# In-projection of a hybrid SSD and Hyena layer: change of half by contraction steps over four banks, operands split one by one, and the first weight tiles loaded a stage earlier

## The chip, the cores and the metric

One NeuronCore of a Trainium2 chip runs the whole layer as one program. The metric is the device time of one execution in microseconds (us), lower is better. The engines are TensorE (PE, with its weight loads as PEld), VectorE (DVE), ScalarE (ACT), GpSimd (POOL) and SyncE (SP), which here only issues DMAs. Each engine runs its own instructions strictly in the order of the program and meets the others through semaphores.

## The reference, cut to what matters

The layer normalises its input, multiplies it by one wide weight matrix (the in-projection), and feeds the columns to an SSD mixer and to a long convolution. Only the first three lines below are touched by the change.

```
h  = rmsnorm(x, norm_w) * (1.0 + scale) + shift          # x: 2048 tokens x 1024, f32
hc = rmsnorm(ctx, norm_w) * (1.0 + scale_c) + shift_c    # ctx: 256 tokens
cols = in_projection(h, w_in)                            # 1024 -> 9248 columns
...
y_m = mamba_mixer(cols["m_xbc"], cols["m_dt"], ...)      # width-3 convolution, chunked scan
y_h = hyena_mixer(cols["h_proj"], ...)                   # width-3 convolution, long convolution
out = x + gate * mixer_output(...)
```

## The kernel before

The in-projection (`phase_in_projection`, L513) is computed transposed: weight tiles of 128 output columns stand still in TensorE and 512 tokens stream past. The 2048 tokens are worked in two halves of 1024. A half is a list of NJ = 37 jobs, so `jobs` has 74; job NJ (number 37) is the first one of the second half. All jobs but one take a pair of weight tiles and one step of a Strassen-like scheme: seven products (`PAIR`, L519) instead of eight, each of a weight operand (A11, A12, S2, S3, S1, A22, S4: two plain halves first, the rest tiles or sums) with an operand of the tokens (B11, B21, T2, T3, T1, N4, B22: quarters of the normalised input and their sums and differences). A product has four contraction steps (k = 0 to 3, the constant KQ), and a step has three matmuls of 128x512: high by high (L715), low part of the tokens (L716), low part of the weights (L717), since every f32 operand is split into a rounded high part and the rest. So a pair job is 7 x 4 x 3 = 84 matmuls. The products go round four PSUM banks.

Who does what for a job: SP loads weight tiles into a ring of three (L648). POOL forms the four weight sums (L666 to L671) and then the low parts of all seven weight operands (L678). ACT rounds the high parts (`split`, L743), copies product 0 out of its bank (L808), and applies the closing function to the job before (`finish`, L753 and L763) and issues its store (L766). DVE adds up the other products (`take`, L843 to L859) and does the width-3 convolution of the job before (`conv`, L881 and L885). For jobs without a convolution (the last 16 of a half) `finish` runs when products 3 and 5 of the next job are done.

The token operands are made by the class `Operands` (L287), once per half and in four steps k: SP loads two row blocks of 128x1024 (`load`, L305) into one of two buffers; DVE multiplies by norm weight and by the rows of 1/rms, which lie in PSUM (`scale`, L311); ACT adds the shift (`shift`, L318); POOL forms T1, T3, T2 and N4 (`sums`, L328, L329, L331, L333); ACT rounds the high parts (`high`, L349) and DVE subtracts for the low ones (`low`, L354), both in three groups: B11, then B21 with B22, then the four sums as one instruction over 2048 columns.

For the first half this runs inside the norm stage (`phase_norm`, L357), between the context's own projection (L433). For the second half it runs inside the in-projection at job NJ, and there the raw rows lie in the buffer `pl_raw`, one set of which belongs to the even jobs and one to the odd, and the sums lie in the result buffers `pl_res`. So at job NJ every engine first ends the first half: the first load (SP, L305) waits for the `finish` of job NJ-2, the others for that of NJ-1; DVE and ACT wait until TensorE has done all products of job NJ-1; POOL waits for the last stores out of `pl_res`. TensorE takes product 0 of job NJ through k = 0 to 3, then product 1, and so on, and waits before each step for the group of the operand it needs (`PARTS` and `GROUP`).

Between stages the semaphores are cleared and all engines meet (`Phase.release`, L66 and L67). The first weight tiles of the in-projection are loaded after that meeting.

Of the kernel before, what the change touches and what calls it, by code (L numbers as in the profile page):

```python
# [18 lines left out]
F32 = mybir.dt.float32  # L19
# [267 lines left out]
class Operands:  # L287
# [4 lines left out]
    GROUP = (0, 1, 1, 2, 2, 2, 2)  # L292
    PARTS = 3
# [6 lines left out]

    def load(self, sp, k):
# [19 lines left out]
    def sums(self, pool, k):  # L321
        a, b = self.xb(k % 2, 0), self.xb(k % 2, 1)
        b11, b12, b21, b22 = a[:, 0:QW], a[:, QW:2 * QW], b[:, 0:QW], b[:, QW:2 * QW]
        t1, t2, t3, n4 = (self.tmp[:, i // 2, i % 2] for i in range(4))
        pool.wait_ge(self.s_norm, 2 * k + 2)
        if k:
            pool.wait_ge(self.s_lo, self.PARTS * k)
        self.nc.gpsimd.tensor_tensor(t1, b12, b11, ALU.subtract).then_inc(self.s_sum, 1)  # L328
        self.nc.gpsimd.tensor_tensor(t3, b22, b12, ALU.subtract).then_inc(self.s_sum, 1)  # L329
        pool.wait_ge(self.s_sum, 4 * k + 1)  # L330
        self.nc.gpsimd.tensor_tensor(t2, b22, t1, ALU.subtract).then_inc(self.s_sum, 1)  # L331
        pool.wait_ge(self.s_sum, 4 * k + 3)
        self.nc.gpsimd.tensor_tensor(n4, b21, t2, ALU.subtract).then_inc(self.s_sum, 1)  # L333

    def part(self, k, g):

        a, b = self.xb(k % 2, 0), self.xb(k % 2, 1)
        src = (a[:, 0:QW], b.rearrange("p (a n) -> p a n", a=2), self.tmp[:])[g]
        views = ((lambda o: o[:, 0, k, :]), (lambda o: o[:, 1:3, k, :]),
                 (lambda o: o[:, 3:7, k, :].rearrange("p (a b) n -> p a b n", b=2)))  # L340
        return src, views[g](self.hi), views[g](self.lo)

    def high(self, act, k, g):
        src, hi, lo = self.part(k, g)
        if g < 2:
            act.wait_ge(self.s_norm, 2 * k + g + 1)
        else:
            act.wait_ge(self.s_sum, 4 * k + 4)
        self.nc.scalar.activation(hi, src, ACT.Copy).then_inc(self.s_hi, 1)  # L349

    def low(self, dve, k, g):
        src, hi, lo = self.part(k, g)
        dve.wait_ge(self.s_hi, self.PARTS * k + g + 1)
# [3 lines left out]
def phase_norm(nc, t, keep, rs, op_hi, op_lo, xbc_c, dt_c):  # L357

    NW = 2 * KT + 1
    with ExitStack() as ctx:  # L360
# [9 lines left out]
        tmp = ph.sb("tmp", [P, 2, 2, QW])  # L370
# [7 lines left out]
                       lambda q, r: xb[:, q, r, :], tmp)  # L378
# [4 lines left out]
        def _(sp):  # L383
# [22 lines left out]
            for n in range(NW):  # L406
# [4 lines left out]
                if n in (4, 8):  # L411
                    ops.load(sp, n // 4 + 1)
            store(NW - 2)
# [23 lines left out]
        def _(act):  # L437
# [10 lines left out]
            for n in range(NW):  # L448
                act.wait_ge(s_mm, n + 1)
                if n < 2 * KT:  # L450
# [6 lines left out]
                    elif n % 4 == 1:  # L457
                        ops.high(act, k, 0)
# [2001 lines left out]
```

## Time and profile before

| what | us |
|---|---|
| median of 3 runs | 3803.88 (3801.89 to 3812.24) |
| profiled execution, its time | 3812.66 |
| profiled execution, its span | 3810.5 |
| in-projection in the span | 162.1 to about 1669 |
| TensorE busy in the span | 3419.6 (90%) |

All times of rows are positions in the span of the profiled execution. What lies around the span is 2.2 us. That execution is 8.8 us slower than the median, so differences are read off the profile and then taken from the median. A matmul's row shows a modelled duration: where matmuls follow one another what counts is the distance of their starts, which is 0.227 us at the full clock and 0.427 us at half of it.

### The profile page before, as it was taken

How to read it: one execution, taken by the hardware profiler on the slowest of the kernel's cores; microseconds unless marked ns; L12 is line 12 of the kernel's file. 1: busy time of each engine (PE TensorE's matmuls, PEld its weight loads, DVE VectorE, ACT ScalarE, POOL GpSimd, SP SyncE). 2: the span in 40 equal slices, each digit the busy share in tenths (PEclk: the TensorE clock that was granted, in tenths of full speed). 3: DMA queues.
4: the chain of work that ended last, by engine and by line, in shares of the span. 5: the costliest groups of instructions: out<-in, count | busy, mean ns of one | idle time of the engine just before them, and what ended most of it. 6: DMA issues, size and time to landing. Idle time of an engine off the chain costs nothing. (4 is left out here: it accounts for less than half of the span.)

```text
span 3810.5 us, 44950 instructions
## 1 busy us (share of the span) xinstructions
PE 3419.6 (90%) x16246; PEld 2827.6 (74%) x16246; DVE 2272.3 (60%) x2870; ACT 1523.0 (40%) x2933; POOL 1864.7 (49%) x1146
## 2 busy tenths in 40 slices
PE   6799999995999999966998999999577887999998
PEld 2678888884788888854996888887366776788886
DVE  5686885223778852227543666665576675567662
ACT  3423223334332223331775555454346553333332
POOL 0477998775869987721000101100257562445442
PEclk8899999997999999988999999999798998999999
DMA  7444333333343333358997857865594545556562
GB/s 255 154 139 143 116 111 111 111 111 110 105 143 106 111 111 111 111 201 345 279 298 201 186 129 172 183 158 130 178 376 144 161 137 186 171 194 209 184 200 100
DMA packets 406350, 636.47 MB, mean 167 GB/s; under 512 B 154731, under 2 KB 241691, under 8 KB 403091
## 3 DMA queue, kind: packets, MB, share of 16 engines
q1 hardware_dynamic: 305661, 442.22, 38.0%
q10 hardware_dynamic: 91256, 157.83, 11.3%
q0 software_dynamic: 9216, 33.56, 4.0%
q8 instruction: 132, 2.16, 0.3%
q14 instruction: 85, 0.70, 0.1%
HBM read 430.49 MB, written 203.03 MB: 166 GB/s over the span
## 5 line engine op out<-in xcount | busy, mean ns | idle before, releaser
L715 PE MATMUL pl_bank<-hl_hi,pl_a_hi 128*128 128x512 f32 x2056 | 811.9, 395 | 69.6 <-DVE hl_lo L354 47.0
L717 PE MATMUL pl_bank<-hl_hi,pl_a_lo 128*128 128x512 f32 x2056 | 804.2, 391 | 0.0
L716 PE MATMUL pl_bank<-hl_lo,pl_a_hi 128*128 128x512 f32 x2056 | 803.8, 391 | 0.0
L715 PEld LDWEIGHTS pl_bank<-hl_hi,pl_a_hi 128*128 128x128 f32 x2056 | 388.1, 189 | 152.8 <-DVE hl_lo L354 39.2
L678 POOL TENSOR_TENSOR pl_a_lo<-pl_sums,pl_a_hi 128x512 fp32r<-128x512 f32 x288 | 435.5, 1523 | 129.3 <-ACT pl_a_hi L743 129.2
L717 PEld LDWEIGHTS pl_bank<-hl_hi,pl_a_lo 128*128 128x128 f32 x2056 | 388.1, 189 | 82.2
L716 PEld LDWEIGHTS pl_bank<-hl_lo,pl_a_hi 128*128 128x128 f32 x2056 | 388.6, 189 | 78.5
L743 ACT ACTIVATE pl_a_hi<-pl_sums 128x512 fp32r<-128x512 f32 x288 | 181.9, 633 | 511.6 <-PE pl_bank L717 464.2
L2022 POOL TENSOR_TENSOR mo_w_lo<-mo_w,mo_w_hi 128x1024 fp32r<-128x1024 f32 x96 | 237.5, 2477 | 280.5 <-ACT mo_w_hi L2093 280.5
L678 POOL TENSOR_TENSOR pl_a_lo<-pl_w,pl_a_hi 128x512 fp32r<-128x512 f32 x220 | 306.8, 1408 | 102.6 <-ACT pl_a_hi L743 102.3
L2050 PE MATMUL mo_bank<-mo_hi,mo_w_hi 128*128 128x512 f32 x768 | 306.8, 400 | 23.4 <-POOL mo_w_lo L2022 18.6
L885 DVE SCALAR_TENSOR_TENSOR pl_res<-pl_raw,pl_taps,pl_res 128x1023 f32<-128x1023 f32 (+1 forms) x160 | 312.6, 1954 | 3.0
L2051 PE MATMUL mo_bank<-mo_lo,mo_w_hi 128*128 128x512 f32 x768 | 301.5, 393 | 0.0
L2052 PE MATMUL mo_bank<-mo_hi,mo_w_lo 128*128 128x512 f32 x768 | 301.4, 392 | 0.0
L1393 DVE TENSOR_TENSOR conv_prod<-conv_bank,conv_spec 128x512 f32<-128x512 f32 x256 | 173.1, 689 | 160.5 <-PE conv_bank L1286 132.2
L743 ACT ACTIVATE pl_a_hi<-pl_w 128x512 fp32r<-128x512 f32 x220 | 138.0, 629 | 293.2 <-PE pl_bank L717 284.5
L1346 ACT COPY conv_v<-conv_bank 128x256 f32<-128x256 f32 x256 | 154.2, 602 | 223.6 <-PE conv_bank L1297 223.6
L1205 POOL DMA_DIRECT2D conv_gin<-u_s x32 | 36.7, 1150 | 382.1 <-DVE conv_x L1358 382.1
L1198 POOL DMA_DIRECT2D conv_x<-u_s x16 | 18.6, 1162 | 385.6 <-POOLq L67 264.3
L2050 PEld LDWEIGHTS mo_bank<-mo_hi,mo_w_hi 128*128 128x128 f32 x768 | 145.4, 189 | 59.1 <-issue 18.5
L1111 DVE COPY spec_y<-spec_bank 64x256 f32<-64x256 f32 x256 | 109.4, 427 | 120.5 <-PE spec_bank L1085 118.5
L843 DVE TENSOR_TENSOR pl_raw<-pl_bank,pl_r 128x512 f32<-128x512 f32 x72 | 49.8, 692 | 209.7 <-PE pl_bank L717 183.5
(247 smaller groups left out, 7049.9 us busy)
## 6 DMA issues: line engine op xcount, KB each, us to landing
pl_w<-in_w_rec SPq DMA_DIRECT2D x146, 512.0 KB, 3.5
conv_spec<-spec_s SPq DMA_DIRECT2D x248, 256.0 KB, 6.0
mo_w<-in_w_br SPq DMA_DIRECT2D x96, 512.0 KB, 3.8
kern_s<-taps_res SPq DMA_DIRECT2D x16, 2048.0 KB, 7.0
spec_xin<-kern_s SPq DMA_DIRECT2D x64, 512.0 KB, 5.4
spec_s<-spec_res ACTq DMA_DIRECT2D x128, 256.0 KB, 4.0
st_xb<-tok_s SPq DMA_DIRECT2D x36, 768.0 KB, 7.2
g_s<-pl_res ACTq DMA_DIRECT2D x32, 512.0 KB, 3.0
```

The source lines that it names most:

```text
L678: nc.gpsimd.tensor_tensor(a_lo[:, n % NS, :], s, a_hi[:, n % NS, :].bitcast(F32), ALU.subtract).then_inc(s_lo, 1)
L715: pe.matmul(out, a_hi[:, q, m], op_hi[:, b, k, :], start=(i == 0 and k == 0), stop=False)
L716: pe.matmul(out, a_hi[:, q, m], op_lo[:, b, k, :], start=False, stop=False)
L717: mm = pe.matmul(out, a_lo[:, q, m], op_hi[:, b, k, :], start=False, stop=(i == len(terms) - 1 and k == KQ - 1))
L743: nc.scalar.activation(a_hi[:, n % NS, :], src, ACT.Copy).then_inc(s_hi, 1)
L885: nc.vector.scalar_tensor_tensor(out=dst, in0=src[:, i:i + width], scalar=taps[i], in1=dst, op0=ALU.mult, op1=ALU.add).then_inc(s_conv, 1)
L1346: nc.scalar.copy(v[:, :, k], bank[2 + k % 2][:, 0:CB]).then_inc(s_vm, 1)
L1393: nc.vector.tensor_tensor(prod[:, n % 4], bank[ubank[k % 4]][:, None, 0:CB].to_broadcast([P, 2, CB]), spec[:, n // 2 % SLOT, :, k % 2], AL ...
L2022: nc.gpsimd.tensor_tensor(w_lo[:, s % 3, :], w[:, s % 3, :], w_hi[:, s % 3, :].bitcast(F32), ALU.subtract).then_inc(s_wlo, 1)
L2050: pe.matmul(bank[s % 4][:], w_hi[:, q, m], hi[:, slot, k, :], start=(k == 0), stop=False)
L2051: pe.matmul(bank[s % 4][:], w_hi[:, q, m], lo[:, slot, k, :], start=False, stop=False)
L2052: mm = pe.matmul(bank[s % 4][:], w_lo[:, q, m], hi[:, slot, k, :], start=False, stop=(k == KT - 1))
```

## The change

Seven edits, all around the two seams of the in-projection (its start, and the change of half at job NJ):

1. The first two weight tiles go to a buffer outside both stages (`first`, `loaded`) and SP loads them near the end of the norm stage, ahead of its last two stores.
2. In job 0 POOL makes the low parts of A11 and A12 ahead of the four weight sums.
3. The token operands are split one at a time: seven `high` and seven `low` of 128x512 per step k, in the order of `ORDERS`, and each waits for its own sum only.
4. At job NJ TensorE takes products 0 to 3 together, step by step: step k = 0 of all four (into four banks), then k = 1, and so on. Products 4 to 6 follow as before.
5. `finish` of jobs without a convolution moves to products 0 and 1 of the next job.
6. Step k = 0 of the second half's operands moves ahead, into job NJ-1: load after the `finish` of NJ-2, `scale` behind product 3, `shift` behind product 4, splits behind products 5 and 6.
7. The sums lie in `pl_tok`, so that POOL waits for older stores. POOL does them for k = 0 between the low parts S3 and S1 of job NJ. A load may overwrite its buffer once the sums and the low part of B22 are done.

The core of the diff (the norm stage splits by the same rule and is left out):

```diff
@@ class Operands
     def load(self, sp, k):
         if k >= 2:
-            sp.wait_ge(self.s_lo, self.PARTS * (k - 1))
+            sp.wait_ge(self.s_sum, 4 * (k - 1))
+            sp.wait_ge(self.s_lo, self.count(k - 2, self.B22))
@@ phase_norm, SP
+            for i in range(2):
+                sp.dma_start(first["w"][:, i, :], t["w_rec"][T_XBC + i]).then_inc(first["s_w"][i], 16)
             store(NW - 2)
             store(NW - 1)
@@ phase_in_projection, SP
                 if J == NJ + 1:
                     sp.wait_ge(s_fin, fin0[NJ - 1])
                     ops.load(sp, 0)
                     sp.wait_ge(s_fin, fin0[NJ])
+                    sp.wait_ge(s_ed, ed0[NJ])
                     for k in range(1, KQ):
                         ops.load(sp, k)
@@ TensorE
+                if J == NJ:
+                    for k in range(KQ):
+                        for j in range(4):
+                            n = p0[J] + j
+                            (a, b), = prods[j]
+                            if k == 0:
+                                room(n)
+                                pe.wait_ge(s_lo, a0[J] + a + 1)
+                            mm = step(J, n, a, b, k, k == 0, k == KQ - 1)
@@ ScalarE
                 if J == NJ:
+                    act.wait_ge(s_mm, p0[NJ])
                     for m in order(J - 1):
                         finish(J - 1, m)
-                    act.wait_ge(s_mm, p0[NJ])
-                    ops.shift(act, 0)
...
+                    for i in (4, 5, 6):
+                        ops.high(act, 0, i)
+                    ops.shift(act, 1)
+                    for k in range(1, KQ):
+                        for i in range(5):
+                            ops.high(act, k, i)
                         if k + 1 < KQ:
                             ops.shift(act, k + 1)
-                        ops.high(act, k, 2)
+                        for i in (5, 6):
+                            ops.high(act, k, i)
...
+                    if J == NJ - 1:
+                        if j == 4:
+                            ops.shift(act, 0)
+                        for i in {5: (0, 1), 6: (2, 3)}.get(j, ()):
+                            ops.high(act, 0, i)
@@ VectorE
+                    if J == NJ - 1:
+                        if j == 3:
+                            ops.scale(dve, 0)
+                        for i in (0, 1, 2, 3) if j == 6 else ():
+                            ops.low(dve, 0, i)
```

ACT around the end of the first half, before: `pl_a_hi` are weight splits, L763 is `finish`, L318 `shift`, L349 `high`.

```order
453 L763 ACTIVATE pl_res<-pl_raw 128x1024
454 L766 DMA g_s<-pl_res 128x1024
455 L743 ACTIVATE pl_a_hi<-pl_sums 128x512
456 L763 ACTIVATE pl_res<-pl_raw 128x1024
457 L766 DMA g_s<-pl_res 128x1024
458 L763 ACTIVATE pl_res<-pl_raw 128x1024
459 L766 DMA g_s<-pl_res 128x1024
460 L318 ACTIVATE pl_raw<-pl_raw,keep_mod 128x1024 x2
461 L349 ACTIVATE hl_hi<-pl_raw 128x512
462 L349 ACTIVATE hl_hi<-pl_raw 128x2x512
463 L318 ACTIVATE pl_raw<-pl_raw,keep_mod 128x1024 x2
464 L349 ACTIVATE hl_hi<-pl_res 128x4x512
```

The same place now (L819 is `finish`, L324 `shift`, L369 `high`, L799 the weight split):

```order
455 L819 ACTIVATE pl_res<-pl_raw 128x1024
456 L822 DMA g_s<-pl_res 128x1024
457 L799 ACTIVATE pl_a_hi<-pl_sums 128x512 x3
458 L324 ACTIVATE pl_raw<-pl_raw,keep_mod 128x1024 x2
459 L799 ACTIVATE pl_a_hi<-hl_w 128x512
460 L369 ACTIVATE hl_hi<-pl_raw 128x512 x2
461 L799 ACTIVATE pl_a_hi<-pl_sums 128x512
462 L369 ACTIVATE hl_hi<-pl_tok 128x512 x2
463 L819 ACTIVATE pl_res<-pl_raw 128x1024
...
465 L819 ACTIVATE pl_res<-pl_raw 128x1024
...
467 L369 ACTIVATE hl_hi<-pl_tok 128x512 x2
```

The `shift` of k = 0 and four splits now stand among the weight splits of the last job of the half; the two closing `finish` stand between the splits of T1, T3 and those of T2, N4.

POOL at the same change of half, before: L678 makes low parts of weights, L328 to L333 the sums of a step.

```order
325 L678 TENSOR_TENSOR pl_a_lo<-pl_w,pl_a_hi 128x512 x2
326 L678 TENSOR_TENSOR pl_a_lo<-pl_sums,pl_a_hi 128x512 x3
327 L678 TENSOR_TENSOR pl_a_lo<-pl_w,pl_a_hi 128x512
328 L678 TENSOR_TENSOR pl_a_lo<-pl_sums,pl_a_hi 128x512
329 L328 TENSOR_TENSOR pl_res<-pl_raw 128x512
```

And now (L696 the low parts, L340 to L348 the sums):

```order
326 L696 TENSOR_TENSOR pl_a_lo<-pl_sums,pl_a_hi 128x512 x2
327 L340 TENSOR_TENSOR pl_tok<-pl_raw 128x512
328 L342 TENSOR_TENSOR pl_tok<-pl_raw 128x512
329 L345 TENSOR_TENSOR pl_tok<-pl_raw,pl_tok 128x512
330 L348 TENSOR_TENSOR pl_tok<-pl_raw,pl_tok 128x512
331 L696 TENSOR_TENSOR pl_a_lo<-pl_sums,pl_a_hi 128x512
332 L696 TENSOR_TENSOR pl_a_lo<-hl_w,pl_a_hi 128x512
333 L696 TENSOR_TENSOR pl_a_lo<-pl_sums,pl_a_hi 128x512
334 L340 TENSOR_TENSOR pl_tok<-pl_raw 128x512
```

The sums of k = 0 went ahead of three low parts; the sums of k = 1 to 3 follow after them.

POOL in job 0 of the in-projection, before and then now:

```order
32 L666 TENSOR_TENSOR pl_sums<-pl_w 128x512
33 L668 TENSOR_TENSOR pl_sums<-pl_sums,pl_w 128x512
34 L669 TENSOR_TENSOR pl_sums<-pl_w 128x512
35 L671 TENSOR_TENSOR pl_sums<-pl_w,pl_sums 128x512
36 L678 TENSOR_TENSOR pl_a_lo<-pl_w,pl_a_hi 128x512 x2
```

```order
32 L696 TENSOR_TENSOR pl_a_lo<-hl_w,pl_a_hi 128x512 x2
33 L691 TENSOR_TENSOR pl_sums<-hl_w 128x512
34 L691 TENSOR_TENSOR pl_sums<-pl_sums,hl_w 128x512
35 L691 TENSOR_TENSOR pl_sums<-hl_w 128x512
36 L691 TENSOR_TENSOR pl_sums<-hl_w,pl_sums 128x512
```

The two low parts that TensorE's first two products need moved ahead of the four sums.

## Rows read from the trace of the kernel before

**Rows 1.** Windows: length, busy us (count) of PE, PEld, DVE, ACT, POOL, clock, DMA.

```profile
162.00:175.50 13.50, 0.00 (x0) 0.00 (x0) 0.38 (x11) 3.96 (x7) 6.30 (x6) 0.50 0.38 129
175.50:897.80 722.30, 717.87 (x3204) 591.85 (x3204) 421.51 (x447) 224.15 (x339) 593.54 (x403) 1.00 0.34 117
897.80:957.10 59.30, 12.34 (x34) 8.06 (x33) 30.61 (x22) 26.72 (x26) 30.78 (x20) 0.59 0.34 124
```

**Rows 2.** Waits, 897 to 975 us: total us, times, longest.

```profile
PE pl_bank L715 <- DVE hl_lo L354: 47.0, 5, 12.0
```

**Rows 3.** Waits of SP's queue, 880 to 1000 us.

```profile
SPq L305 <- ACT pl_res L763: 30.4, 2, 26.8
```

**Rows 4.** Timeline of PE, change of half: start, us, instruction, idle before and releaser.

```profile
897.60 0.39 PE L717 MATMUL pl_bank<-hl_hi,pl_a_lo 128*128 128x512 f32 x1
908.39 0.77 PE L715 MATMUL pl_bank<-hl_hi,pl_a_hi 128*128 128x512 f32 x1 [10.40 <-DVE hl_lo L354]
...
946.41 0.80 PE L715 MATMUL pl_bank<-hl_hi,pl_a_hi 128*128 128x512 f32 x1 [11.99 <-DVE hl_lo L354]
```

**Rows 5.** Timeline of the same stretch, the other engines.

```profile
884.43 0.69 DVE L843 TENSOR_TENSOR pl_raw<-pl_bank,pl_r 128x512 f32<-128x512 f32 x1 [4.75 <-PE pl_bank L717]
...
895.93 1.05 ACT L763 ACTIVATE pl_res<-pl_raw 128x1024 f32<-128x1024 f32 x1
...
903.34 2.47 DVE L311 SCALAR_TENSOR_TENSOR pl_raw<-pl_raw,keep_mod,rt_rows 128x1024 f32<-128x1024 f32 x2 [4.62 <-DMA pl_raw<-in_xT]
904.72 2.28 ACT L318 ACTIVATE pl_raw<-pl_raw,keep_mod 128x1024 f32<-128x1024 f32 x2 [3.33 <-DVE pl_raw L311]
...
907.55 0.69 DVE L354 TENSOR_TENSOR hl_lo<-pl_raw,hl_hi 128x512 fp32r<-128x512 f32 x1 [1.73 <-ACT hl_hi L349]
...
908.50 1.22 DVE L354 TENSOR_TENSOR hl_lo<-pl_raw,hl_hi 128x1024 fp32r<-128x1024 f32 x1 [0.25 <-ACT hl_hi L349]
...
910.82 1.27 POOL L329 TENSOR_TENSOR pl_res<-pl_raw 128x512 f32<-128x512 f32 x1
...
918.84 2.90 DVE L354 TENSOR_TENSOR hl_lo<-pl_raw,hl_hi 128x512 fp32r<-128x512 f32 x2
919.07 1.59 POOL L328 TENSOR_TENSOR pl_res<-pl_raw 128x512 f32<-128x512 f32 x1 [4.41 <-DVE hl_lo L354]
...
920.62 2.24 POOL L329 TENSOR_TENSOR pl_res<-pl_raw 128x512 f32<-128x512 f32 x1
...
971.88 0.69 DVE L859 TENSOR_TENSOR pl_raw<-pl_bank,pl_u 128x512 f32<-128x512 f32 x1 [2.03 <-PE pl_bank L717]
```

**Rows 6.** DMA issues in four short windows: KB each, us to landing.

```profile
xbc_c<-nl_res SPq DMA_DIRECT2D x1, 128.0 KB, 4.6
...
dt_c<-nl_res SPq DMA_DIRECT2D x1, 128.0 KB, 1.8
...
pl_ident<-in_ident SPq DMA_DIRECT2D x1, 64.0 KB, 2.6
...
pl_raw<-in_xT SPq DMA_DIRECT2D x2, 512.0 KB, 5.4
```

**Rows 7.** Timeline, norm stage to in-projection.

```profile
162.98 18.93 SPq L648 DMA_DIRECT2D pl_w<-in_w_rec  x5
167.72 1.15 ACT L743 ACTIVATE pl_a_hi<-pl_w 128x512 fp32r<-128x512 f32 x2 [8.72 <-DMA pl_w<-in_w_rec]
169.12 1.26 POOL L666 TENSOR_TENSOR pl_sums<-pl_w 128x512 f32<-128x512 f32 x1 [19.64 <-DMA pl_w<-in_w_rec]
...
175.53 0.76 PE L715 MATMUL pl_bank<-hl_hi,pl_a_hi 128*128 128x512 f32 x1 [22.63 <-POOL pl_a_lo L678]
...
181.64 0.40 PE L717 MATMUL pl_bank<-hl_hi,pl_a_lo 128*128 128x512 f32 x1
```

**Rows 8.** Source lines L67 and L66: duration ns min/median/max, first and last start.

```profile
L67 SPq EVENT_SEMAPHORE  x10: 17/17/17, 81.6 to 3810.5; - x10
...
L66 POOLq DRAIN  x10: 58/98/121, 81.0 to 3809.8; - x10
```

More of the change, by code:

```diff
@@ L664, in _ @@
+                if not J:
+                    low(A11, half[0][0])
+                    low(A12, half[0][1])
                 if len(job.tiles) == 2:
-                    n = 4 * pairs[J]
-                    nc.gpsimd.tensor_tensor(sums[:, 0], wt[1][:, 0:QW], wt[1][:, QW:D], ALU.add).then_inc(s_sum, 1)
+                    total(0, half[1][0], half[1][1], ALU.add)
                     pool.wait_ge(s_sum, n + 1)
-                    nc.gpsimd.tensor_tensor(sums[:, 1], sums[:, 0], wt[0][:, 0:QW], ALU.subtract).then_inc(s_sum, 1)
@@ L675, in _ @@
-                for i, s in enumerate(src):
-                    n = a0[J] + i
-                    pool.wait_ge(s_hi, n + 1)
-                    nc.gpsimd.tensor_tensor(a_lo[:, n % NS, :], s, a_hi[:, n % NS, :].bitcast(F32), ALU.subtract
-                                            ).then_inc(s_lo, 1)
+                    total(3, half[0][1], sums[:, 1], ALU.subtract)
+                if J:
+                    low(A11, half[0][0])
+                    low(A12, half[0][1])
+                if len(job.tiles) == 2:
+                    low(S2, sums[:, 1])
+                    low(S3, sums[:, 2])
+                    if J == NJ:
+                        for q in range(2):
+                            pool.wait_ge(s_tst[q], 16 * stores_before(t0[NJ] + q))
+                        ops.sums(pool, 0)
+                    low(S1, sums[:, 0])
+                    low(A22, half[1][1])
+                    low(S4, sums[:, 3])
@@ L700, in _, with room, step @@
             pe.wait_ge(s_ident, 16)
-            for J, prods in enumerate(products):
+            def room(n):
+                if n >= 4:
+                    engine, count = freed[n - 4]
+                    pe.wait_ge(s_ea if engine == "act" else s_ed, count)
+            def step(J, n, a, b, k, begin, end):
+                out, q, m = bank[n % 4][:], (a0[J] + a) % NS, slice(k * P, (k + 1) * P)
+                if J == NJ:
+                    pe.wait_ge(ops.s_lo, ops.count(k, b))
+                pe.matmul(out, a_hi[:, q, m], op_hi[:, b, k, :], start=begin, stop=False)
+                pe.matmul(out, a_hi[:, q, m], op_lo[:, b, k, :], start=False, stop=False)
+                return pe.matmul(out, a_lo[:, q, m], op_hi[:, b, k, :], start=False, stop=end)
@@ L810, in _ @@
                         split(J + 1, j)
[L811 to L814 removed]
+                    if J and J != NJ:
+                        for m in order(J - 1):
+                            if j == (5 - 2 * m if jobs[J - 1].conv is not None else 1 - m):
+                                finish(J - 1, m)
+                    if J == NJ - 1:
[3 more added lines that the diff above has]
+                            ops.high(act, 0, i)
                     if j == 2 and J >= 2 and jobs[J - 2].turned:
```

152 lines of the change are left out of this document (81 added, 71 removed).

## The prediction

> **What bounds the kernel now.** I read the windows by stage first, then who waited for whom, then the timelines of the two stretches in which TensorE stands still. Within a half TensorE is the bound: between 175.5 and 897.8 us it is busy 717.87 of 722.30 us at the full clock, matmuls 0.227 us apart, while POOL is busy 82% of it and DVE 58% [rows 1]. No faster helper pays there. What can be saved lies at two seams.
>
> Seam A, the start: from 162.0 to 175.5 TensorE does nothing [rows 1]. The weights are issued at 162.98, ACT gets them at 167.72, POOL makes four sums from 169.12 and only then, near 174.1, the first low part, and the first matmul comes at 175.53, at half clock (0.427 us a matmul) until 181.64 [rows 7].
>
> Seam B, the change of half: the last matmul of the first half starts at 897.60 and ends its slot at 897.83 [rows 4]. The 84 matmuls of job NJ at 0.227 us would end 19.1 us later, at 916.9. The last product is taken by DVE at 971.88 [rows 5], so it ended at about 971.7: the seam costs 54.8 us. 47.0 us of it are five waits for DVE's low parts [rows 2], and the granted clock of the stretch is 0.59, the lower level while TensorE waits [rows 1]. It takes the steps k one after another because product 0 needs all four; they come at 908.39 to 946.41, 12.7 us apart [rows 4].
>
> **Seam A, part by part.** The first two tiles are already there when the stage opens, so what is left is: ACT's two high parts (0.65 us for the first; 1.15 for both [rows 7]), POOL's first low part (1.27, as a POOL subtraction without disturbance [rows 5]), and the identity matrix, on whose DMA TensorE waits ahead of everything: issued just ahead of the weights of 162.98, say 162.5, 2.6 us to landing [rows 6, 7], so 165.1. The first two end at 162.2 + 0.65 + 1.27 = 164.2; the identity is late next, so TensorE starts at 165.2 if the stage opens when it does now. The sums, now behind two low parts, are ready in time: POOL has low parts A11 at 164.2, A12 at 165.5, sums until 170.6, S2 at 171.9; TensorE wants S2 after 24 matmuls, 14 of them at half clock, 165.2 + 8.3 = 173.5. Cover: 1.6 us.
> The two weight loads stand ahead of the last two stores of the norm stage in SP's queue, and the stage ends when these have landed. Now they take 1.8 us; a store behind 1.5 MB of loads took 4.6 us [rows 6]. Here 1 MB is issued at about 156 and wants 5.4 us by the row of a pair of loads [rows 6], until 161.4; the last store, issued near 158.5, lands at about 161.8 instead of 161.2. I take a stage that opens 0.5 us later; bounds are 1 us earlier (one-by-one splits free DVE and ACT for the convolution before the last sooner, so the last stores go out sooner) and 2.5 us later (the 4.6 us in full). The splits themselves are the same work in more pieces, 28 instead of 12 on each engine, beside TensorE; I put them at nothing, with 1 us either way inside the same bounds.
> By the Trainium skill, DMA: Bandwidth & Descriptors, Queues, rings and completion order, descriptors of one issuing engine are consumed in ring order on each DMA engine. That speaks against putting the loads ahead of the stores; the 4.6 us row agrees with it, and the sum by the rule alone would be the late bound.
> Gain of seam A: 175.5 - 165.7 = 9.8 us (7.8 to 11.3). The cold start is the same in both.
>
> **Seam B, part by part.** Products end 2.72 us apart, product 1 of job NJ-1 at 884.4 [rows 5].
> 1. Load 0 waits for the second `finish` of NJ-2, now ended at 896.98 [rows 5]. At product 1 it ends at 884.4 + 0.65 (split) + 1.05 = 886.1. SP has stood there since 897.0 - 26.8 = 870 [rows 3], nothing else is queued ahead. The rows land 6.3 us later (897.0 to 903.34 [rows 5]) at 892.4.
> 2. `scale` takes 2.47, `shift` ends 3.7 after its start [rows 5]: 896.1. DVE stands for the load ahead of the take of product 4 (until 894.9 instead of 892.6); that bank is wanted again only by product 1 of job NJ, so nothing waits. POOL has low part S3 done at 892, makes T1 by 897.4 and T3 by 898.6.
> 3. DVE's low parts start behind its last take, 898.7, at 0.7 to 0.97 us: B11 by 899.6, B21 900.5, T1 and T3 by 902.3. TensorE works on products 0 and 1 there, 1.8 us after its end of the first half.
> 4. ACT's two closing `finish` (1.05 and a DMA issue, 1.5 each) stand ahead of T2: they run 899.9 to 902.5. T2 is split at 903.5, its low part is there at 904.3.
> 5. Load 1 waits for both: 902.5, landing 5.4 to 6.3 us later [rows 5, 6], 908.3. From here three steps are left, as now, but they no longer wait in series for one instruction of 2048 columns.
> 6. One step: `scale` and `shift` 3.7 us, then POOL. POOL and DVE disturb each other when both work on two SBUF operands: DVE's two instructions took 2.90 us at 918.84 where 0.69 + 1.22 = 1.9 is undisturbed, and POOL's two beside them 1.59 + 2.24 instead of 2 x 1.27; beside L311, whose one operand is in PSUM, POOL keeps its 1.27 (910.82) [rows 5]. So each loses about half of the overlap. Step 1: normalised at 912.0, T1 and T3 made after 2.54 + 1.4 = 916.0, T3 rounded at 916.7, then `shift` of step 2 (2.3) until 919.3. N4 of step 1 is made by 918.6; only then may load 3 go, 5.4 us, 924.0; behind DVE's five low parts `scale` starts 924.5, and step 3 is normalised at 928.2. T1, T3, T2 of it take 3.8 + 2.1, the high and the low part 1.3: T2 of step 3 is there at 935.4. The pitch is 8.1 us instead of 12.7.
> 7. TensorE has then 6 + 36 matmuls left. It has had bursts of 3 to 6 between waits, so I take the lower clock, which the whole stretch shows now (0.59 granted on the mean [rows 1]), and for as long as after 175.53: 6.1 us, 14 matmuls [rows 7]: 14 x 0.427 + 28 x 0.227 = 12.3 us. End at 947.8 instead of 971.7.
> Gain of seam B: 23.9 us. Bounds: with no disturbance at all the last T2 comes at 931.5 (gain 28); with today's pitch of 12.7 for steps 2 and 3, behind T2 of step 1 at 920.8, at 946.2 (gain 13). The value taken is the one whose terms are rows of this stretch.
> By the Trainium skill, GPSIMD Engine Reference, its specification table, the two engines contend when DVE has two SBUF inputs; the rows of point 6 agree. Were it a full exclusion, 4.2 + 5.1 = 9.3 us a step, the gain would be about 21.
>
> What is queued behind: POOL turns to job NJ+1 at about 936.3 and has A11 after four sums and a low part, 6.6 us, 942.9; TensorE wants it at 947.8. Cover 4.9 us (now 11). In steady jobs POOL has slack, and TensorE never waits for it, so the lead grows back. The earlier `finish` costs ACT 2.64 us in product 0's 2.72 us, ahead of nothing TensorE waits for. I put both at nothing.
> **A new cost:** the weight semaphores now belong to an outer group, which had none, so one more clear and meeting stands behind the in-projection: 81.0 to 81.6 [rows 8], 0.6 us.
>
> **Sum:** -9.8 - 23.9 + 0.6 = -33.1 us. From the profiled execution 3812.66 that gives 3779.6. It was 8.8 us above the median of the runs, so for the median I say 3803.88 - 33.1 = 3770.8.
>
> **Rivals.** (a) The pitch stays: splits one by one bring more instructions and semaphore trips, POOL and DVE fill the time, steps come 12.7 us apart. For it: DVE and ACT waited for each other in every step. Against: most of each step now is idle, DVE is busy 30.6 of 59.3 us [rows 1]. -9.8 - 13 + 0.6 = 3781.7.
> (b) Both better than taken: disturbance and stage end cost nothing, 28 + 11.3 - 0.6: 3765.2.
> (c) The preload pays little: the last stores wait behind the weights and the identity behind them, seam A gives 5: 3775.6.
> (d) Slower: POOL, which comes out of seam B with 4.9 us of lead instead of 11, does not regain it in the 20 jobs with a convolution, and sets their pace. It decides from 33.1/20 = 1.7 us a job; at 2.3 us the time is 3817. Against: in the first half the same jobs start with little lead and TensorE lost 4.4 of 722 us [rows 1].
>
> **How the numbers follow.** The forecast 0.74, (a) 0.12, (b) 0.07, (c) 0.04, (d) 0.03. The forecast's own terms give 3766 to 3779, and the median of a few runs moves by some us (the three lie 10 apart). I take 3763 to 3784, which holds (a), (b) and (c). Faster by over 0.3% (11 us, about what a measurement of this kernel tells from no change) 0.96, same 0.01, slower 0.03.
>
> **What would show it.** First matmul of the in-projection at 165 to 167; load 0 issued near 886; TensorE in pairs of bursts, the last long wait ending near 935; end of job NJ near 948; waits for the low parts of the tokens in that stretch 20 to 27 us instead of 47; no waits for POOL in jobs NJ+1 to NJ+3. I am wrong if load 0 is late, so that DVE delays the takes, if the steps keep 12.7 us, or if the norm stage ends over 2 us later.

## The result, and the profile after

The changed kernel takes 3788.04 us (median of 5, 3785.08 to 3793.64) against 3804.16 of the kernel before beside it: ratio 0.9950, interval 0.9939 to 0.9961, so 15 to 23 us less. The forecast was 33 us less, 3770.8, and its range ended at 3784. The sign was right and the size was not.

Windows of the changed kernel, as [rows 1]: opening of the in-projection to its first matmul, the first half, and from its end to the last long wait of TensorE.

```profile
160.90:163.41 2.51, 0.00 (x1) 0.00 (x1) 0.35 (x11) 1.15 (x2) 1.70 (x2) 0.50 0.49 101
163.41:886.10 722.69, 717.87 (x3204) 591.81 (x3204) 423.63 (x449) 230.00 (x348) 598.03 (x407) 1.00 0.35 120
886.10:935.00 48.90, 19.26 (x43) 10.74 (x43) 44.82 (x35) 25.22 (x38) 35.00 (x23) 0.64 0.34 118
```

The first half is what it was (722.7 us, 3204 matmuls). In the last window DVE is busy 44.8 of 48.9 us; before it was 30.6 of 59.3. TensorE's waits there, as [rows 2]:

```profile
PE pl_bank L750 <- DVE hl_lo L374: 29.6, 10, 6.0
```

Where the in-projection opens and ends, by the semaphore that lets SP out of the meeting between stages (first and last start), in the changed kernel:

```profile
L67 SPq EVENT_SEMAPHORE  x3: 17/17/17, 160.8 to 1649.0; - x3
```

Before, the same two meetings lie at 162.0 and 1673.2. The norm stage and the in-projection together took 1591.6 us and take 1568.7 now, 22.9 less; the new meeting costs 0.4 (1648.6 to 1649.0). All stages behind it took 2137.3 us and take 2136.3.

**Seam A.** Timeline of the changed kernel, as [rows 7]:

```profile
156.41 0.43 SPq L415 DMA_DIRECT2D dt_c<-nl_res  x1
...
160.91 1.15 ACT L799 ACTIVATE pl_a_hi<-hl_w 128x512 fp32r<-128x512 f32 x2 [4.89 <-PEq L67]
161.27 0.42 SPq L656 DMA_DIRECT2D pl_ident<-in_ident  x1
161.71 2.49 POOL L696 TENSOR_TENSOR pl_a_lo<-hl_w,pl_a_hi 128x512 fp32r<-128x512 f32 x2 [14.39 <-ACT pl_a_hi L799]
...
163.41 0.79 PE L750 MATMUL pl_bank<-hl_hi,pl_a_hi 128*128 128x512 f32 x1 [12.66 <-DMA pl_ident<-in_ident]
```

The identity matrix is what comes last, as forecast, and the first matmul comes 2.6 us after the stage opens instead of 13.5. The norm stage's last store, `dt_c`, takes 3.4 us to landing where it took 1.8, but it is issued 1.3 us sooner in its stage, so that the stage is 0.5 us longer.

**Seam B.** I count from the end of the first half (the first wait's end less its length: 887.70 - 1.47 = 886.2; before 908.39 - 10.40 = 898.0) to the start of DVE's take of the last product of job NJ. That was 971.88 - 898.0 = 73.9 us and is 61.4. Timeline of the changed kernel, DVE and POOL in the last step; L317 is `scale`, L374 `low`, L340 to L348 the four sums of the step, L691 and L696 weight sums and weight low parts of job NJ+1:

```profile
917.64 2.46 DVE L317 SCALAR_TENSOR_TENSOR pl_raw<-pl_raw,keep_mod,rt_rows 128x1024 f32<-128x1024 f32 x2
...
920.02 1.28 DVE L374 TENSOR_TENSOR hl_lo<-pl_tok,hl_hi 128x512 fp32r<-128x512 f32 x2
...
924.78 5.15 DVE L374 TENSOR_TENSOR hl_lo<-pl_raw,hl_hi 128x512 fp32r<-128x512 f32 x3
...
926.15 1.54 POOL L348 TENSOR_TENSOR pl_tok<-pl_raw,pl_tok 128x512 f32<-128x512 f32 x1
927.65 1.74 POOL L691 TENSOR_TENSOR pl_sums<-hl_w 128x512 f32<-128x512 f32 x1
...
929.47 1.59 POOL L691 TENSOR_TENSOR pl_sums<-pl_sums,hl_w 128x512 f32<-128x512 f32 x1
929.86 6.76 DVE L374 TENSOR_TENSOR hl_lo<-pl_tok,hl_hi 128x512 fp32r<-128x512 f32 x4
931.02 1.70 POOL L691 TENSOR_TENSOR pl_sums<-hl_w 128x512 f32<-128x512 f32 x1
932.69 1.71 POOL L691 TENSOR_TENSOR pl_sums<-hl_w,pl_sums 128x512 f32<-128x512 f32 x1
934.36 3.40 POOL L696 TENSOR_TENSOR pl_a_lo<-hl_w,pl_a_hi 128x512 fp32r<-128x512 f32 x2
...
936.55 0.68 DVE L907 TENSOR_TENSOR pl_raw<-pl_bank,pl_r 128x512 f32<-128x512 f32 x1
```

At 920.02 POOL rests and two low parts take 1.28 us. From 929.86 POOL works without a gap and four take 6.76, 1.69 each. POOL's instructions start 1.67 us apart there; earlier, beside nothing of DVE but takes out of PSUM, they start 1.25 us apart:

```profile
884.41 1.29 POOL L340 TENSOR_TENSOR pl_tok<-pl_raw 128x512 f32<-128x512 f32 x1 [4.23 <-ACT pl_raw L324]
885.66 1.28 POOL L342 TENSOR_TENSOR pl_tok<-pl_raw 128x512 f32<-128x512 f32 x1
```

A pair (one low part and one POOL instruction) takes 1.68 us. Both alone add up to 1.25 + 0.60 = 1.85, so only 0.17 us of the two overlap.

My theory after reading this, called **turn-taking** below: a DVE and a POOL instruction that both read two operands from SBUF do not share, they go one after the other, whole (but for these 0.17 us). The price of a low part beside a busy POOL is then one POOL instruction, whatever its own size, and splitting the operands one by one bought up to seven such turns in a step where there had been three. The rivals: the share goes by columns, as the forecast had it; ScalarE's highs or the loads set the pace; the interleaving over four banks, or the early freeing of the raw rows, carries the gain.

### The profile page after: what moved, and what is told of

It reads as the page before. It is cut to its first block and busy times, and to the rows that moved or that the text cites. A ratio compares the mean times of both kernels' runs of the same rounds, so it can differ in the third digit from the quotient of the medians.

```text
span 3785.4 us, 45041 instructions
## 1 busy us (share of the span) xinstructions
PE 3424.3 (90%) x16246; PEld 2828.8 (75%) x16246; DVE 2295.8 (61%) x2902; ACT 1525.8 (40%) x2965; POOL 1867.0 (49%) x1146
## 3 DMA queue, kind: packets, MB, share of 16 engines
q10 hardware_dynamic: 91256, 157.83, 11.2%
## 5 line engine op out<-in xcount | busy, mean ns | idle before, releaser
L750 PE MATMUL pl_bank<-hl_hi,pl_a_hi 128*128 128x512 f32 x2056 | 813.6, 396 | 42.3 <-DVE hl_lo L374 29.6
L696 POOL TENSOR_TENSOR pl_a_lo<-pl_sums,pl_a_hi 128x512 fp32r<-128x512 f32 x288 | 436.0, 1526 | 120.9 <-ACT pl_a_hi L799 120.9
L799 ACT ACTIVATE pl_a_hi<-pl_sums 128x512 fp32r<-128x512 f32 x288 | 181.8, 633 | 541.6 <-PE pl_bank L752 485.4
L696 POOL TENSOR_TENSOR pl_a_lo<-hl_w,pl_a_hi 128x512 fp32r<-128x512 f32 x220 | 309.8, 1422 | 115.5 <-ACT pl_a_hi L799 115.2
L2121 PE MATMUL mo_bank<-mo_hi,mo_w_hi 128*128 128x512 f32 x768 | 306.7, 399 | 22.5 <-POOL mo_w_lo L2093 18.4
L799 ACT ACTIVATE pl_a_hi<-hl_w 128x512 fp32r<-128x512 f32 x220 | 138.1, 629 | 259.1 <-PE pl_bank L752 253.2
L691 POOL TENSOR_TENSOR pl_sums<-hl_w 128x512 f32<-128x512 f32 x144 | 208.5, 1448 | 12.2 <-POOL pl_a_lo L696 12.2
L2121 PEld LDWEIGHTS mo_bank<-mo_hi,mo_w_hi 128*128 128x128 f32 x768 | 145.2, 189 | 58.7 <-issue 18.6
```

Source lines behind the costliest of these rows:

```text
L691: nc.gpsimd.tensor_tensor(sums[:, i], x, y, op).then_inc(s_sum, 1)
L696: nc.gpsimd.tensor_tensor(a_lo[:, at % NS, :], src, a_hi[:, at % NS, :].bitcast(F32), ALU.subtract).then_inc(s_lo, 1)
L750: pe.matmul(out, a_hi[:, q, m], op_hi[:, b, k, :], start=begin, stop=False)
L799: nc.scalar.activation(a_hi[:, n % NS, :], src, ACT.Copy).then_inc(s_hi, 1)
L2121: pe.matmul(bank[s % 4][:], w_hi[:, q, m], hi[:, slot, k, :], start=(k == 0), stop=False)
```

## Experiments

Time ratios are to the kernel before on the same chip. Norm stage and in-projection are the stages' lengths in the profile, in us. "Last wait" is the start of the matmul behind TensorE's last wait for a low part, and "seam B" the end of job NJ, both from the end of the first half. Stops under 0.3 us are left out of "last wait": the low part of T2 of the last step is taken at 44.8 with the sums by VectorE, and at 48.7 product by product.

| kernel | ratio (95%) | norm stage | in-projection | last wait | seam B |
|---|---|---|---|---|---|
| before | 1 | 80.4 | 1511.2 | 59.1 | 73.9 |
| changed | 0.9950 (0.9939-0.9961) | 80.9 | 1487.8 | 48.8 | 61.4 |
| changed, again | 0.9950 (0.9935-0.9964) | 80.7 | 1488.0 | 48.8 | 61.3 |
| seam A alone | 0.9979 (0.9969-0.9988) | 81.8 | 1499.8 | 58.7 | 73.4 |
| seam B alone | 0.9959 (0.9944-0.9974) | 79.4 | 1496.7 | 48.7 | 61.2 |
| late freeing | 0.9944 (0.9926-0.9963) | 81.0 | 1488.4 | 50.8 | 62.5 |
| product by product | 0.9944 (0.9924-0.9965) | 80.9 | 1486.0 | 40.2 | 60.6 |
| low parts in halves | 0.9973 (0.9963-0.9984) | 80.8 | 1491.6 | 53.0 | 65.6 |
| POOL waits | 0.9927 (0.9911-0.9942) | 82.0 | 1480.4 | 44.4 | 54.3 |
| POOL waits, again | 0.9936 (0.9923-0.9948) | 81.1 | 1482.4 | 44.4 | 55.9 |
| sums by VectorE | 0.9927 (0.9915-0.9940) | 81.1 | 1480.5 | 41.8 | 55.1 |
| both edits | 0.9925 (0.9911-0.9938) | 80.9 | 1477.6 | 41.1 | 51.0 |
| both edits, again | 0.9930 (0.9918-0.9942) | 81.2 | 1477.3 | 41.2 | 51.0 |
| both, product by product | 0.9937 (0.9922-0.9952) | 81.4 | 1482.6 | 38.1 | 56.9 |

**The two seams apart.** Seam A alone is the kernel before with the two tiles loaded in the norm stage, and in job 0:

```diff
+                if not J:
+                    for i, s in enumerate((wt[0][:, 0:QW], wt[0][:, QW:D])):
+                        pool.wait_ge(s_hi, i + 1)
+                        nc.gpsimd.tensor_tensor(a_lo[:, i, :], s, a_hi[:, i, :].bitcast(F32), ALU.subtract
+                                                ).then_inc(s_lo, 1)
```

> The kernel before, and of the change only the first seam: the first two weight tiles are loaded in the norm stage and job 0's low parts A11 and A12 are made ahead of its four weight sums; the change of half is as before. Theory: the first matmul of the in-projection comes 83.5 us after the meeting that opens the norm stage's last part instead of 93.9, all later jobs keep their length (722.6 for the first half, 73.9 from the end of the half to the end of job NJ), and the time is 10 us under the kernel before, 3794. Rival (the gain of the first seam is given back later, by loads of weight tiles that now stand elsewhere in the queue or by a later stage that waits for something else): under 5 us.

Seam B alone is the changed kernel without that:

```diff
-            for i in range(2):
-                sp.dma_start(first["w"][:, i, :], t["w_rec"][T_XBC + i]).then_inc(first["s_w"][i], 16)
...
-                if not J:
-                    low(A11, half[0][0])
-                    low(A12, half[0][1])
```

> The changed kernel without its part at the first seam: no weight tile is loaded in the norm stage, and in job 0 POOL makes its four weight sums ahead of A11 and A12, as in the kernel before. Theory: the two parts are independent; the first matmul comes 93.9 us after the meeting that opens the norm stage's last part, job NJ ends 61.4 us after the end of the half, and the time is 12.5 us under the kernel before, 3793. Rival (the two seams share something, and the sum of the parts is not the whole): with the 8 us that the first seam alone gave beside a gain of the whole of 19 us, this one would then give clearly less or more than 11.

In the profiles the first alone saves 10.0 us of norm stage and in-projection, the second 15.5, together 25.5 where the whole change saves 22.9 (22.9 in its repeat: 80.7 + 1488.0). Seam B itself is 61.2 alone and 61.4 in the whole, and the first matmul stands 3.0 us after the opening in the one with seam A, 12.8 in the one without. So the parts are independent, within what such stages scatter: the norm stage without preload took 79.4 and 80.4, with it 80.7 to 82.0. By times the parts give 8 us (5 to 12) and 16 us (10 to 21), and the whole 19 (15 to 23). By these single profiles the norm stage holds two effects that nearly cancel: the loads make it 1.4 us longer (seam A alone against the kernel before; 1.3 to 1.5 for the whole against seam B alone), and the splits one by one 1.0 shorter (seam B alone against the kernel before).

> The changed kernel once more, unaltered, beside the parts. In the two profiles its seams give 10.4 + 12.5 - 0.4 = 22.5 us, its times 16 to 19 us. If the profiles tell it rightly, the ratio to the kernel before is 0.9941 and the profile repeats 83.5 us to the first matmul and 61.4 us to the end of job NJ; if the rest of the program takes some of it back, the ratio is 0.995 to 0.996 and the stages behind the in-projection are longer than before.

The profile repeats to 0.2 us, and so does the ratio, at the end that speaks for something taken back. The profile doesn't show it: the stages behind the in-projection took 2137.3 us before, 2136.3 and 2137.9 with the change, and 2133.0 to 2142.3 over all kernels here, which don't alter them. Whether 22.5 or 19 is the gain stays open; both lie in the interval. Of the 13 profiles behind the first row of the table, 12 show a larger gain of the two stages than the times do, by 1 to 9 us and 3 to 4 on average. All are counted from the one profile of the kernel before, but that profile is not long where it can be compared: its first half, seam B and the rest of its in-projection are within 0.5 us of those of seam A alone.

**What carries seam B.** Late freeing:

```diff
         if k >= 2:
             sp.wait_ge(self.s_sum, 4 * (k - 1))
-            sp.wait_ge(self.s_lo, self.count(k - 2, self.B22))
+            sp.wait_ge(self.s_lo, self.PARTS * (k - 1))
```

> The changed kernel with another of its parts undone: the load of step k waits until VectorE has made all seven low parts of step k-2, no longer only those that read the raw rows. Theory: VectorE sets the pitch of the steps, and a load has slack: load 2 would land at some 903 us of the profile, where its scaling starts at 906.5 anyway; load 3 would be issued at 913.7 and land 6.2 us later at 919.9, where its scaling starts at 917.6 now: the last wait ends 2.3 us later, 51.2 us after the end of the half, the time is 2 us more. Rival (the early freeing carries most of what the seam gained): each of the two loads delays its step by all of the time between the low part of B22 and that of N4, 7 us, and the time is 10 us more or above.

The last wait ended 2.0 us later, as the slack of the loads says, and the time did not tell it. By the profile the early freeing is worth 1 to 2 us at the seam.

Product by product:

```diff
-                if J == NJ:
+                if False:
                     for k in range(KQ):
...
-                    if J == NJ and j < 4:
-                        continue
```

> The changed kernel with one of its parts undone: TensorE takes the first four products of job NJ one after the other, each over its four contraction steps, as in the kernel before; order of the operands, freeing of the raw rows and the second job's loads stay. Theory: what ends the last wait is the last low part of the last step (T2), which both orders need; only the matmuls left behind it differ, 51 instead of 42 of 0.22 us: the last wait ends at 48.9 us as now, job NJ ends at 63.4 us after the half's end instead of 61.4, the time is 2 us more. Rival (the interleaving over four banks carries most of what the seam gained): job NJ ends at 68 to 74, as in the kernel before (73.9), and the time is 7 to 12 us more.

The last long wait of this kernel, on the timeline of TensorE, is for B11 of the last step:

```profile
926.99 0.80 PE L750 MATMUL pl_bank<-hl_hi,pl_a_hi 128*128 128x512 f32 x1 [9.45 <-DVE hl_lo L374]
```

The rival fell, and my sum too: job NJ ended 0.8 us sooner, not 2 later. Behind that wait stand 75 matmuls, 20.4 us. The first 24 keep TensorE busy for 8.2 us, and 0.25 us later the low part of T2 is there; the 51 behind T2 ran at the full clock, 11.7 us, while the 42 of the interleaved order came out of a wait of 5.74 us and began at half of it, 12.6 us. In the changed kernel the interleaving over four banks is worth nothing.

What the 12.5 us consist of can be read from the scalings (`scale`), again from the end of the half. Before, those of steps 1, 2 and 3 start at 11.7, 26.4 and 40.0; now at 11.4, 20.3 and 31.4. So of the 12.5 us 8.3 lie between the scalings of step 1 and step 3, 1.8 from there to the last wait's end, and 2.2 behind it. Step 0 was moved ahead by 11.0 us, and step 1 starts only 0.3 sooner. How much of the 8.3 us, beyond the early freeing, comes from splitting one by one and how much from having step 0's splits out of the way was not run apart.

**What sets the pace.** Low parts in halves, for the steps after the first:

```diff
+        if self.cut and k:
+            h = QW // 2
+            for r in (slice(0, h), slice(h, QW)):
+                ins = self.nc.vector.tensor_tensor(lo[:, r], src[:, r], hi[:, r].bitcast(F32), ALU.subtract)
+                ins.then_inc(self.s_lo if r.start else self.s_cut, 1)
```

> The changed kernel, and in the steps after the first of the second half each low part of VectorE is made by two instructions of 256 columns instead of one of 512: the same columns, twice the instructions. Theory (turn-taking): where POOL has work for as many turns as VectorE has instructions (the last step, where it goes on to job NJ+1), each of the 7 further instructions pays one more POOL turn or a good part of it, up to 1.2 us: the last wait for hl_lo ends 5 to 6 us later and job NJ ends 67 us after the half's end instead of 61.4; in the two steps before, POOL has only its four sums to make, so little changes. Rival (the share of SBUF goes by columns): the same columns take the same time, only the fixed part of an instruction comes on top, some 0.06 us each: 0.5 us at the seam, job NJ ends at 62.

Timeline of this kernel, last step (the row of five from the view of 928 to 934.3):

```profile
921.09 1.42 DVE L380 TENSOR_TENSOR hl_lo<-pl_tok,hl_hi 128x256 fp32r<-128x256 f32 x4
...
927.40 7.14 DVE L380 TENSOR_TENSOR hl_lo<-pl_raw,hl_hi 128x256 fp32r<-128x256 f32 x5
...
931.40 1.46 POOL L700 TENSOR_TENSOR pl_sums<-hl_w 128x512 f32<-128x512 f32 x1
932.82 1.45 POOL L700 TENSOR_TENSOR pl_sums<-hl_w,pl_sums 128x512 f32<-128x512 f32 x1
```

Alone a half takes 0.36 us (1.42 / 4), a little over half of the 0.62 to 0.64; beside POOL it takes 1.43 (7.14 / 5) against 1.69. Half the columns, and 85% of the price: what POOL adds is 1.07 us to either size, and the share by columns is out. Job NJ ended 4.2 us later, 65.6, nearer to the 67 of turn-taking than to the 62 of the rival; the time is above that of the changed kernel too (0.9973 against 0.9950, intervals apart). I had put too much of it in the last step (2.6 us) and too little in the two before (1.6), where POOL's sums meet more low parts than I counted.

POOL waits:

```diff
                 if J == NJ:
                     for k in range(1, KQ):
                         ops.sums(pool, k)
+                    pool.wait_ge(ops.s_lo, B.PARTS * KQ)
```

> The changed kernel, and in the second half POOL, when it has made the last step's four sums, waits until VectorE has made the last low part of the half before it turns to the weight sums and low parts of job NJ+1. Theory (turn-taking): a VectorE instruction with two operands in SBUF and a POOL instruction of the same kind do not share, they take turns whole, so that a 512-column low part costs 0.53 + 1.17 = 1.7 us while POOL has work and 0.6 us while it has none. In the last step POOL's last four turns are then gone: the last four low parts take 0.6 us each, TensorE's last wait for hl_lo ends 44 us after the half's end instead of 48.9, job NJ ends at 56.7 instead of 61.4, and the time falls by 4 to 5 us against the changed kernel. Rival (ScalarE's highs, or a share of SBUF that goes by columns, set the pace of the last step): the last wait ends where it did, within 1 us, and the time is the changed kernel's; POOL's weight sums of job NJ+1 come later, in the 12 us of matmuls that are left, and cost nothing.

Timeline of this kernel at the same place:

```profile
925.04 4.05 DVE L374 TENSOR_TENSOR hl_lo<-pl_raw,hl_hi 128x512 fp32r<-128x512 f32 x3
926.39 1.55 POOL L348 TENSOR_TENSOR pl_tok<-pl_raw,pl_tok 128x512 f32<-128x512 f32 x1
...
929.01 2.49 DVE L374 TENSOR_TENSOR hl_lo<-pl_tok,hl_hi 128x512 fp32r<-128x512 f32 x4
931.42 0.68 DVE L908 TENSOR_TENSOR pl_raw<-pl_bank,pl_r 128x512 f32<-128x512 f32 x1
931.58 1.29 POOL L691 TENSOR_TENSOR pl_sums<-hl_w 128x512 f32<-128x512 f32 x1 [3.64 <-DVE hl_lo L374]
```

The four low parts that took 6.76 us take 2.49, with ScalarE, loads and operands unaltered. The last wait ended at 44.4 (forecast 44). It is one line, and it makes POOL do the same work later, where TensorE has 42 matmuls left: 5 to 9 us of time by the two ratios, whose intervals still touch that of the changed kernel, and 7.4 and 5.4 us of the in-projection. Seam B fell by more than the 4.4 us, because the granted clock behind the last wait was the upper one. Windows of TensorE behind the last wait, in the changed kernel and in this one (length, busy, clock):

```profile
935.00:938.00 3.00, 3.00 (x7) 0.50 0.00 0
```

```profile
930.95:933.95 3.00, 3.00 (x13) 1.00 0.00 0
```

In the repeat the same wait of 1.44 us was followed by the lower clock, and seam B was 55.9:

```profile
931.60:934.60 3.00, 3.00 (x7) 0.52 0.00 0
```

> POOL's wait alone once more, unaltered: ratio 0.9927 as before, in-projection 1480.4 us, job NJ ends 54.3 us after the end of the half; some 3 us above the version with both edits if a difference of the in-projection reaches the time.

Sums by VectorE (and the tiles of job NJ+1 issued behind load 0):

```diff
-        self.nc.gpsimd.tensor_tensor(t1, b12, b11, ALU.subtract).then_inc(self.s_sum, 1)
+        engine.tensor_tensor(t1, b12, b11, ALU.subtract).then_inc(self.s_sum, 1)
...
+                        ops.sums(dve, k, nc.vector)
                         for i in range(3):
                             ops.low(dve, k, i)
```

> The changed kernel, and in the second half the four sums of each step (T1, T3, T2, N4) are made by VectorE instead of POOL; SP issues the weight tiles of job NJ+1 behind load 0 already, so that POOL can make that job's sums while VectorE waits for loads. Theory (turn-taking: a low part costs 1.7 us beside a POOL instruction and 0.6 us alone): VectorE has four instructions more in each step, but each of its eleven takes 0.6 us, so a step takes 2.4 + 11 x 0.6 = 9.0 us of VectorE instead of 11.1; the last step has no POOL turn in it. TensorE's last wait ends about 40 us after the end of the half instead of 48.9, job NJ ends at 50 to 52 instead of 61.4, the time is 9 to 10 us under the changed kernel, 3778. Rival (the cost of a low part does not come from POOL, it is the load of the memory by any engine): each step takes 4 x 0.6 = 2.4 us more of VectorE than now, 13.5 us, and the time is 5 to 7 us above the changed kernel.

VectorE has four instructions more in each step and seam B is 6.3 us shorter, so the rival fell. It stayed 3 to 5 us behind the theory; 3.7 us of this is that step 1 began late: in step 0 VectorE's sums met POOL's work for job NJ+1, the last take came at 890.49, load 1 waited for it until 893.88, and its scaling began 15.1 us after the end of the half instead of 11.4.

Both edits: the sums of steps 1 to 3 by VectorE, and POOL's wait.

> The changed kernel with the two edits that helped, put together so that neither starts late: step 0 of the second half as in the changed kernel (POOL makes its sums, load 1 ahead of all weight tiles, so that its scaling starts 11.4 us after the end of the half and not 15.1 as when VectorE made all sums), the sums of steps 1 to 3 by VectorE, and POOL waits for the last low part before it turns to the weight sums of job NJ+1. Theory (turn-taking): from the scaling of step 1 on everything keeps the distances that it had with VectorE's sums (8.1, 9.8 us between the scalings, 8.9 us from the last scaling to the wait that ends last), so the last wait ends at 11.4 + 8.1 + 9.8 + 8.8 = 38.1 us instead of 48.8, job NJ ends at 51 instead of 61.4, and the time is 10 us under the changed kernel, 3777, 3 us under either edit alone. Rival (the start of step 1 is not what either edit alone was short of, ScalarE's shifts or the order of PE's products take over): job NJ ends at 54 to 55 as with either edit alone and the time is theirs.

Timeline of this kernel, last step: four sums, seven low parts, nothing beside them:

```profile
921.50 0.69 DVE L341 TENSOR_TENSOR pl_tok<-pl_raw 128x512 f32<-128x512 f32 x1
...
924.10 1.89 DVE L375 TENSOR_TENSOR hl_lo<-pl_raw,hl_hi 128x512 fp32r<-128x512 f32 x3
925.91 2.49 DVE L375 TENSOR_TENSOR hl_lo<-pl_tok,hl_hi 128x512 fp32r<-128x512 f32 x4
...
928.48 1.30 POOL L692 TENSOR_TENSOR pl_sums<-hl_w 128x512 f32<-128x512 f32 x1 [32.56 <-DVE hl_lo L375]
```

Seam B is 51.0 as forecast, though the last wait ended at 41.1 and not 38.1, so the number came out by luck, by two errors that cancel: I had taken the distance to a wait that isn't the last (T2's low part was taken at 44.8 in the kernel with VectorE's sums, 11.7 us behind the scaling of step 3, as here), and for the matmuls behind it the lower clock, where the full one was granted.

> The version with both edits once more, unaltered, beside the one with POOL's wait alone. By the profiles its in-projection is 10.2 us shorter than the changed kernel's and 2.8 us shorter than that of POOL's wait alone. If that reaches the time, the ratio to the kernel before is 0.9920 to 0.9925 and its median lies some 3 us under the other's; if not, the two are equal.

The in-projection is 3 to 5 us shorter than with POOL's wait alone, and the two medians lie 1.8 us apart with intervals that overlap: by time the two are not told apart. Either is 5 to 10 us below the changed kernel.

> The version with both edits (sums of steps 1 to 3 by VectorE, POOL waits), and TensorE takes the first four products of job NJ one after the other again. In the changed kernel that cost nothing: there 84 matmuls stood behind the first low part of the last step, 20.4 us with the first twelve at half the clock, and ended when the low part of T2 came anyway. Theory: now that the low parts come 8 us earlier, the matmuls that are left set the end. The low part of B11 of the last step is there 38 us after the end of the half, and 84 matmuls behind it take 19.2 us at the full clock and 20.4 with twelve at half of it: job NJ ends at 57 to 59 instead of 51, and the time is 6 to 8 us more than that of the version with both edits. Rival (the interleaving is worth nothing here either, since both orders wait for the same low part): job NJ ends within 2 us of 51.

Job NJ ended at 56.9 instead of 51.0: now that the low parts come earlier, the 75 matmuls behind B11 (18.7 us; the expectation's 84 is all of the job) set the end, and the interleaving is worth 5.9 us at the seam (5.0 of the in-projection). The medians differ by 1 to 2 us the same way, with intervals that overlap; the 6 to 8 us of time that I expected did not come.

## Why the forecast was wrong

- **Seam A** was right. The forecast had 9.8 us: a start 10.3 us sooner after the opening, less 0.5 of a longer norm stage. The profile has 13.5 - 2.6 = 10.9, less 0.5 (80.4 to 80.9): 10.4. The last to come is the identity, as named. The half microsecond is about the difference that the forecast worked with: the last store took 3.4 us to landing behind the loads (forecast 3.3, before 1.8) and was issued 1.3 us sooner (forecast 0.9).
- **The new meeting** costs 0.4, forecast 0.6.
- **Seam B, points 1 to 5** were right within 2 us. From the end of the half: load 0 goes out at -11.9 (forecast -11.7), its scaling starts at -5.6 (-5.4), the wait for T2 of step 0 ends at 8.2 (6.5), the scaling of step 1 starts at 11.4 (10.5).
- **Point 6 failed.** From the scaling of step 1 to that of step 3 it had 16.2 us, and these took 20.0; from there to the low part of T2 it had 10.9, and this took 17.4. With 0.9 from the start that is the whole of the 11.2 us by which the last wait was late. The wrong term is "each loses about half of the overlap", taken from one pair of instructions in [rows 5], 2.90 us where 1.9 was undisturbed. Read as turns, that row says: two DVE instructions, one POOL instruction waited for. I carried the loss as a share to a step with seven DVE instructions, and put a low part at 0.7 to 0.97 us where it takes 1.7 beside POOL.
- **What POOL does next was left out.** I had POOL turn to job NJ+1 at 936.3, 38.5 us after the end of the half and 0.9 behind T2's low part, the last that TensorE waits for. It did so at 927.65, 41.4 us after the end of the half, the moment its last sum was made; VectorE was late by more, and T2's low part came 7.4 us behind that. All of the last step's four low parts of the sums then stood beside POOL. That is 4.4 of the 11.2 us, by the kernel in which POOL waits. With VectorE's sums the two steps take 18.0 and the last part 11.7: together the two edits take away 7.7 of the 11.2 us. Seam B comes to 51.0 then, where the forecast had 50.0 for the changed kernel, but not by the forecast's terms: the last wait still ends 3.5 us later than forecast, and the matmuls behind it take 9.9 us instead of 12.3.
- Weighed in the forecast was that the two engines might exclude each other fully, with 9.3 us a step and a gain of 21. The exclusion holds and the gain is 12.5: that sum took four sums and seven low parts once each, and left out POOL's next job and the chain through VectorE, whose `scale` of the next step stands behind the low parts. The Trainium skill, SBUF — State Buffer, section SBUF: two separate sides, says that between a DVE instruction with two SBUF inputs and a GpSimd one that reads SBUF, whichever starts first keeps the shared ports for the whole instruction while the other blocks. The traces agree but for 0.17 us a pair: 1.68 us, where 1.25 and 0.60 are the prices alone.
- **Point 7**, 12.3 us for the last 42 matmuls, was right (12.6), at the lower clock behind the wait of 5.74 us.
- **The bounds.** The low end of the gain of seam B, 13 us, was today's pitch of 12.7 with rival (a). The pitch was shorter (8.8 and 11.1 us), and the gain still 12.5, since the last step grew. Rival (a) named the mechanism, "POOL and DVE fill the time", and was given 0.12. DVE at 44.8 of 48.9 us shows that it was close to the truth on seam B: the argument against it, that most of a step was idle, counted busy time at undisturbed prices.
- **What the seams leave open.** By the profiles the sum is -10.4 - 12.5 + 0.4 = -22.5 us where the forecast had -33.1; seam B's 11.4 us (the 11.2 and 0.2 behind the last wait) are more than that whole miss. Taken from the median before, 22.5 us would have given 3781.4, still inside the range. The measured 3788.04 lies outside because the time gained 16 to 19 us only; where these 3 to 6 us went is the open end named above. TensorE's waits for the tokens' low parts were 29.6 us, above the 20 to 27 that were named as a sign.
- **Cover.** No job behind the seam waits for POOL. Its first low part for job NJ+1 is there 11.3 us before TensorE wants it (forecast 4.9), since the seam ended later than forecast, and 2.6 us before in the kernel where POOL starts after the last low part. Rival (d) is out.

## What to carry to other kernels

Before you cut an instruction into smaller ones, count on which engine the pieces run and what the other of DVE and POOL does meanwhile: beside a busy POOL every piece with two SBUF operands cost the wait for a POOL instruction on top, 1.1 us here, for 512 columns and for 256 alike. Give such a chain to one engine, or let the other wait until it is done if its work has slack; one wait on POOL was worth 5.5 to 7.1 us at the seam, beside the 12.5 of the whole reordering. And when an engine is freed earlier, ask what it takes up next: here that work started at once, beside the low parts that TensorE was waiting for.

## What the runs showed of the hardware

- A 512-column low part takes 0.60 to 0.64 us on DVE alone and 1.69 beside POOL, a 256-column one 0.36 and 1.43; a 512-column POOL instruction starts every 1.25 us alone, every 1.67 beside 512-column low parts and every 1.4 beside 256-column ones. In these pairs the engine with the shorter instruction loses the most.
- The same 42 matmuls took 9.9 us behind a wait of 1.45 us with the clock at 1.00, 11.4 behind one of 1.44 us at 0.52 at first, and 12.6 behind one of 5.74 us at 0.50: waits of the same length on the same kernel were followed by either level. 0.50 is 1.2 GHz, 1.00 is 2.4.
